# Root and reciprocal of four norms on 4 partitions x 128 tokens, spread back into PSUM by products

## What is computed

```
def rms_norm(x, gain=None):
    xf = x.astype(jnp.float32)
    y = xf * lax.rsqrt(jnp.mean(xf * xf, axis=-1, keepdims=True) + EPS)
    ...
def modulate(x, shift, scale):
    return x * (1 + scale) + shift
    ...
    for i in range(DEPTH):
        ax = modulate(rms_norm(hx, norm_mix[i]), sh1, sc1)
        ...
        hx = hx + g1 * yx
        fx = modulate(rms_norm(hx, norm_ffn[i]), sh2, sc2)
        hx = hx + g2 * swiglu(fx, ffn_w1[i], ffn_w3[i], ffn_w2[i])
    ...
        f = jnp.square(jax.nn.relu(h @ w_up[l])) @ w_down[l]
        x = x + rms_norm_2(f, ffn_post_norm[l])
```

## Time and profile before

| | |
|---|---|
| median of 3 runs | 2210.89 us (2209.84 to 2211.0) |
| span of the profiled execution | 2209.8 us |
| TensorE busy | 2159.8 us, 98% |
| VectorE busy | 1174.9 us, 53% |
| ScalarE busy | 752.9 us, 34% |
| granted TensorE clock | nine tenths or more in every one of 40 slices |
| loads and stores | 232.55 MB, 105 GB/s on average |

### The profile page before, as it was taken

How to read it: one execution, slowest core, us unless ns; L and a number is a source line. 1 busy time by engine, 2 the same in 40 slices (tenths; PEclk the granted TensorE clock), 3 DMA queues, 4 the chain that set the end, 5 groups by cost and what they waited for, 6 DMA issues and landing times.

```text
span 2209.8 us, 26001 instructions
## 1 busy us (share of the span) xinstructions
PE 2159.8 (98%) x10000; PEld 1756.9 (80%) x10000; DVE 1174.9 (53%) x1536; ACT 752.9 (34%) x1012; POOL 25.1 (1%) x52
## 2 busy tenths in 40 slices
PE   8999999999999999999999999999989998999998
PEld 4888888888788888878888888888658986888886
DVE  6665646556877323454663233357878657422424
ACT  4332322323522122332332212235665634313322
POOL 0000000000000000000000000000000000000000
PEclk9999999999999999999999999999999999999999
DMA  7342323313377222222222222232101111222221
GB/s 306 112 148 76 131 92 109 114 57 147 115 287 289 103 100 95 77 96 95 96 96 95 95 96 95 95 110 92 64 1 39 39 58 57 95 96 94 96 102 51
DMA packets 33170, 232.55 MB, mean 105 GB/s; under 512 B 3792, under 2 KB 4176, under 8 KB 5840
## 3 DMA queue, kind: packets, MB, share of 16 engines
q1 hardware_dynamic: 26336, 185.62, 23.6%
q0 software_dynamic: 5760, 41.95, 5.1%
q10 hardware_dynamic: 1008, 4.07, 0.5%
HBM read 229.52 MB, written 2.10 MB: 105 GB/s over the span
## 4 chain that ended last, share of the span: by engine, by line
PE 87%; DVE 7%; ACT 3%; issue 2%; DMA 1%; SPq 0%; ACTq 0%; DVEq 0%
PE PS L548 27%; PE PS L549 27%; PE PS L550 27%; DVE normed L1763 1%; PE PS L1076 1%; ACT w_hi L1213 1%; DVE act_lo L1755 1%; PE PS L1066 1%; PE PS L607 1%; DVE w_lo L1742 1%; PE PS L581 1%; DMA x<-x_t 1%; DVE act_lo L1772 0%; DVE rstd L1751 0%; PE PS L911 0%
## 5 line engine op out<-in xcount | busy, mean ns | idle before, releaser
L1742 DVE TENSOR_TENSOR w_lo<-raw,w_hi 128x2048 fp32r<-128x2048 f32 x162 | 371.1, 2291 | 546.0 <-ACT w_hi L1213 545.9
L1213 ACT ACTIVATE w_hi<-raw 128x2048 fp32r<-128x2048 f32 x162 | 310.2, 1915 | 982.6 <-PE PS L550 979.0
L548 PE MATMUL PS<-act_hi,w_hi 128*128 128x512 f32 x1584 | 624.0, 394 | 19.3 <-DVE act_lo L1772 10.1
L550 PE MATMUL PS<-act_hi,w_lo 128*128 128x512 f32 x1584 | 619.0, 391 | 0.0
L549 PE MATMUL PS<-act_lo,w_hi 128*128 128x512 f32 x1584 | 618.9, 391 | 0.0
L548 PEld LDWEIGHTS PS<-act_hi,w_hi 128*128 128x128 f32 x1584 | 298.9, 189 | 89.2 <-issue 15.8
L550 PEld LDWEIGHTS PS<-act_hi,w_lo 128*128 128x128 f32 x1584 | 298.8, 189 | 63.0
L549 PEld LDWEIGHTS PS<-act_lo,w_hi 128*128 128x128 f32 x1584 | 299.2, 189 | 61.8 <-issue 1.0
L548 PE MATMUL PS<-hid_hi,w_hi 128*128 128x512 f32 (+1 forms) x672 | 262.0, 390 | 1.0 <-ACT sg L1700 0.9
L549 PE MATMUL PS<-hid_lo,w_hi 128*128 128x512 f32 (+1 forms) x672 | 261.4, 389 | 0.0
L550 PE MATMUL PS<-hid_hi,w_lo 128*128 128x512 f32 (+1 forms) x672 | 261.4, 389 | 0.0
(11 more groups left out here) (429 smaller groups left out, 2472.7 us busy)
## 6 DMA issues: line engine op xcount, KB each, us to landing
raw<-slabs SPq DMA_DIRECT2D x162, 1024.0 KB, 4.8
ada_raw<-ada POOLq DMA_DIRECT2D x40, 1024.0 KB, 5.0
toep<-decay ACTq DMA_DIRECT2D x4, 768.0 KB, 4.3
early_raw<-ada SPq DMA_DIRECT2D x2, 1024.0 KB, 9.7
x<-x_t SPq DMA_DIRECT2D x2, 1024.0 KB, 10.5
ada_raw<-ada SPq DMA_DIRECT2D x2, 1024.0 KB, 15.5
early_raw<-ada SPq DMA_DIRECT2D x1, 2048.0 KB, 18.7
out_t<-x SPq DMA_DIRECT2D x4, 512.0 KB, 2.8
```

Source lines behind the costliest of these rows:

```text
L548: pe.matmul(o, w[0], a[0], start=first, stop=False)
L550: return pe.matmul(o, w[1], a[0], start=False, stop=last)
L1213: act.activation(w_hi[:, n % 2, :], raw[:, n % 2, :], ACT.Copy).then_inc(w_hi_done, 1)
L1742: dve.tensor_tensor(w_lo[:, k % 2, :], raw[:, k % 2, :], w_hi[:, k % 2, :].bitcast(F32), ALU.subtract).then_inc(w_lo_done, 1)
```

## The change

The sum of squares of the four norms is not spread over all partitions at first. `packed_sum` takes the 512 tokens as 4 groups of 128 and puts group j on partition j of the bank: each of the three products becomes four, with 128 moving columns and a 4-column slice of a small array quarter (zeros with one column of ones) as weights. `packed_root` takes the root of 4 x 128 numbers into root4, `spread_inverse` their reciprocal in place. `spread_root` then spreads each row over 128 partitions with a product of a unit column, broadcast to 128 columns, and puts the inverse into the same PSUM bank, from which VectorE reads it (`inverse`) in y. Since the first slab's tiles are still multiplied by rstd, ScalarE copies the bank to rstd at the head of its `first_pair` (semaphore inverse_kept), and VectorE's `first_pair` waits for that.

Three moves go with it. VectorE's remainder of slab n + 1 no longer stands ahead of the reciprocal but inside `norm_tail`, before the third y. ScalarE squares the last tile before it scales it. ScalarE's rounding of slab n + 1 stands behind the root. At the last norm the spread stands behind the second of TensorE's five x products. Semaphores are merged and renamed (spread_ready, root_inverted) and a padding is cut by the size of the new arrays. The core of the diff, leaving out renamings elsewhere:

```diff
+            def packed_sum(name, b):
+
+                q = nth(name)
+                for k, part in ((5, std[:, :]), (6, sq[:, 0, :]), (7, sq[:, 1, :])):
+                    pe.wait_ge(sq_ready, 8 * q + k + 1)
+                    pe.wait_ge(sq_used, 8 * q + k)
+                    for j in range(TT):
+                        mm = pe.matmul(PS[0:TT, b, 0:P], quarter[:, TT - 1 - j:2 * TT - 1 - j], part[:, j * P:(j + 1) * P],
+                                       start=(k == 5 and j == 0), stop=(k == 7 and j == TT - 1))
+                    mm.then_inc(sq_used, 1)
+
+            def spread_root(name, b):
+
+                pe.wait_ge(root_inverted, RH + packed.index(name) + 1)
+                for j in range(TT):
+                    at = VEC["unit"] + j
+                    mm = pe.matmul(PS[:, b, j * P:(j + 1) * P], vec[0:TT, at:at + 1].to_broadcast([TT, P]), root4[0:TT, :],
+                                   start=True, stop=True)
+                mm.then_inc(spread_ready, 1)
...
                     if s == at_sum:
                         pe.wait_ge(banks, freed[2])
-                        gathered_sum(nth(name), 6)
+                        packed_sum(name, 6)
+                    if s == at_sum + 1:
+                        spread_root(name, 6)
...
                 for k in range(PE_TILES):
+                    if k == 2:
+                        spread_root("last", 7)
                     pe.wait_ge(f_done, FIN.index(k) + 1)
...
+            def packed_root(name, b, bias=eps[0:TT, 0:1]):
+
+                act.wait_ge(sq_used, 8 * nth(name) + 8)
+                act.activation(root4[0:TT, :], PS[0:TT, b, 0:P], ACT.Sqrt, bias=bias, scale=1.0 / D).then_inc(std_ready, 1)
...
             def first_pair(n, seen, step, func=ACT.Silu):
 
+                act.activation(rstd[:, :], bank(6), ACT.Copy).then_inc(inverse_kept, 1)
                 after_static(n)
...
                     act.wait_ge(made, before + s + 1)
-                    scaled(name, s, k)
-                    if s == KT - 1:
-                        after_static(last_slab)
+                    if s < KT - 1:
+                        scaled(name, s, k)
                     square(nth(name), s, x[:, k, :])
-                root(nth(name), T, D, 6)
+                scaled(name, KT - 1, order[KT - 1])
+                packed_root(name, 6)
+                after_static(last_slab)
...
+            def spread_inverse(name, b):
+
+                dve.wait_ge(std_ready, nth(name) + 1)
+                dve.reciprocal(root4[0:TT, :], root4[0:TT, :]).then_inc(root_inverted, 1)
+                dve.wait_ge(spread_ready, nth_spread(name))
+                return bank(b)
...
                 if inverse is None:
-                    inverse = rstd
-                    dve.wait_ge(std_ready, nth(name) + 1)
-                    link(dve.reciprocal(rstd[:, 0:width], std[:, 0:width]))
+                    inverse = spread_inverse(name, 6)
...
+                def second_slab(k):
+
+                    if k == 2:
+                        static_rest(n + 1)
...
             if has("ffn0"):
                 scaled_rest("ffn0", KT - 1, FIN[-1])
-                static_rest(FFN0 + 1)
-                norm("ffn0", 2, 0, 3)
+                norm("ffn0", 2, 0, 3, FFN0)
```

More of the change, by code:

```diff
@@ L393, in build @@
         rope_step = sem("rope_step")
[L394 removed]
+        root_inverted = sem("root_inverted")
         o_scaled = sem("o_scaled")
@@ L399, in build @@
         gathered = ("ffn0", "mix1", "ffn1", "post2", "last")
+        packed = ("ffn0", "mix1", "ffn1", "last")
+        spreads = ["ffn0", "mix1", "ffn1", "final", "pre2", "ffn2", "last"]
         split = ["mix0", "ctx", "ffn0_x", "ffn0", "mix1_x", "mix1", "ffn1_x", "ffn1", "pre2", "ffn2"]
@@ L1976, in head @@
                 dve.wait_ge(ostd_ready, h + 1)
-                dve.reciprocal(rstd[:, :], std[:, :]).then_inc(orstd_done, 1)
-                dve.wait_ge(orstd_done, h + 1)
+                dve.reciprocal(rstd[:, :], std[:, :]).then_inc(root_inverted, 1)
+                dve.wait_ge(root_inverted, h + 1)
                 for e in range(RVT):
@@ L2187, in _ @@
             if has("ffn1"):
-                static_rest(FFN1 + 1)
-                norm("ffn1", 4, 1, 3)
+                norm("ffn1", 4, 1, 3, FFN1)
                 first_pair(FFN1, FT + KT, "ffn1")
@@ L2581, in _ @@
                 dve.wait_ge(f_done, KT)
-                inverse_root("last")
+                inverse = spread_inverse("last", 7)
                 for k in range(KT + 1):
```

71 lines of the change are left out of this document (38 added, 33 removed).

## The result

The changed kernel takes **2214.48 us** (median of 20 runs, 2212.75 to 2215.97), the kernel before 2210.94 us (20 runs, 2209.71 to 2212.58): a ratio of 1.0015 with a 95% interval of 1.0009 to 1.0022. It is slower by 0.15%, within the 0.2% that were called no change. The forecast was 2214.5. The profiled execution spans 2212.0 us against 2209.8, so this one execution is 2.2 us longer while the medians lie 3.5 apart. That difference of 1.3 us became the main question.

The account below looks back on a forecast made before the run. VectorE's train and then ScalarE were taken to set TensorE's restarts. ffn0 1.25, mix1 0.9, ffn1 1.25 and last 0.2 gave +3.6 us, forecast 2214.5 us; own range 2213.3 to 2216.0, overall range 2211.2 to 2217.0.

Parts of the forecast that it names:

- (a): Packed sums at each norm: twelve products of 128 columns replace three of 512, 0.15 us later, bounds 0 and 1.
- (b): ScalarE's root on 4 x 128 at each norm: 0.34 us against 0.69 for 512 columns, bounds 0 and 0.455.
- (c): VectorE's reciprocal on 4 x 128: 0.95 us against 3.35 for 512 columns, cost following columns; bounds 0.35 and 1.75.
- (d): Spread by four TensorE products: 1.16 us until VectorE can read, 0.89 of TensorE's stream; bounds 0.6 and 1.8.
- (e): Slab subtraction moved into VectorE's train before y2: costs 2.08 us, train ends 0.75 later; TensorE's pair still ends before Silu.
- (f): ScalarE's copy of bank 6 to rstd before the slab rounding: 0.50 us, ScalarE being the path from there on.
- (h): VectorE's y reads PSUM instead of SBUF: costs nothing by the rows, 65 ns more per y by the skill.
- the rival on it: PSUM reads stop successive y steps overlapping in VectorE's train at three places: 1.9 us on top, 2216.4 us, chance 0.08.
- dear small products: Rival: packed sums and spread cost 0.6 us more a place, in the chain to y0: 2216.9 us, chance 0.12.
- short chain that is shorter: Rival: reciprocal 0.35 and spread 0.6 bring y0 another 1.15 us forward: about +0.5 us, 2211.4 us, chance 0.10.
- released by TensorE's own pair: Sign of being wrong: waits before the restarts end with TensorE's own pair, not with VectorE's train and then ScalarE.
- The rest that was to be shown: Signs: subtraction between second and third y, TensorE waiting for Silu at ffn0, for subtraction at mix1, no idle before facc.

Follow-up runs that it names:

- moves alone: The kernel before with only VectorE's slab subtraction moved inside the y train, ahead of the third y, at ffn0, mix1 and ffn1: 2217.05 us against 2211.44.
- group 1: Two kernels made from the one before: one with only the moved subtraction, 2217.05 us, one with only the added ScalarE copy, 2212.3 us, both against 2211.44.
- copy alone: The kernel before plus one unread ScalarE copy of PSUM bank 6 at the head of first_pair at ffn0, mix1 and ffn1: 2212.3 us against 2211.44.
- spread first: The changed kernel with the last norm's spread ahead of all five x products instead of behind the second: 2217.14 us against 2210.94 for the kernel before.
- four tiles: The changed kernel with TensorE adding four output tiles instead of five, VectorE the other four: 2213.85 us, ratio 1.0013 to the kernel before.
- three norms: The changed kernel, packed only at ffn0, mix1 and last, old orders, earlier copy, TensorE adding four tiles, unread products at ffn0 and mix1: 2208.7 us against 2211.41.
- moves undone: The changed kernel with the subtraction back ahead of the reciprocal, the slab rounding and last scaled tile back in place: 2211.59 us against 2211.44 for the kernel before.
- copy early: The changed kernel with ScalarE's bank copy between the second and third rounding of act_hi, the third y waiting for it: 2213.31 us against 2211.44.
- two norms: The changed kernel with the root packed at ffn0 and mix1 only, the three old orders back and the copy earlier: 2207.99 us against 2210.94.

## Why the prediction was right, and where it was not

The number and the range held: 2214.48 against 2214.5. By its steps:

- **(a) packed sums.** Forecast 0.15 us later, measured 0.04 (the third sum starts at 568.90 + 1.18 + 0.17 = 570.25 against 570.21), and with the shorter step to the root nothing at all: root at 571.33 against 571.36. The eight passes of four columns cost what the two of 512 do. The term was mis-sized by 0.15.
- **(b), (c), (d) root to y.** Forecast 2.63, measured 2.70: root 0.36 (forecast 0.34), reciprocal 0.94 (0.95), spread 1.15 (1.16). Cost follows the columns, also on four partitions. y0 is 1.44 us earlier; forecast 1.33.
- **(e) the moved subtraction.** Forecast 2.08; moves alone gave 2.08 and 2.06 at ffn0 and ffn1, and 2.46 at mix1, where a longer low clock came on top (group 1). In the changed kernel the train ends 0.61 us later, forecast 0.75, the difference being (a).
- **(f) the copy.** Forecast 0.50, measured 0.48 on ScalarE. But the prediction took ScalarE for the path from there on, as the profile's Silu at the restart suggests, and by the end times it was VectorE's subtraction that held the kernel before, by 0.2 us (group 1). So the term is about 0.3 at ffn0 and ffn1 (0.32 and 0.34 for the copy alone), not 0.50.
- **(h) PSUM reads.** y from PSUM starts its successor after 0.66 us (578.27 to 578.93), as from SBUF. The overhead that the Trainium skill states (Perfetto Trace Analysis, Optimizing Scalar/DVE Operations) is not seen in these rows, and the rival on it falls. So do the dear small products and the short chain that is shorter.
- **The sum.** Forecast 1.25 + 0.9 + 1.25 + 0.2 = 3.6 at the places, measured 0.97 + 0.78 + 0.98 + 0.25 = 2.98, too large by 0.6. Of the 0.28 us at ffn0 about half is the train (0.61 against 0.75) and half the slack that the copy had (0.18).
- **The step that failed** is (e)'s sentence on TensorE: "Its pair took 12.65 us (577.91 to 590.56) and would end near 591.3". The 12.65 us held a stretch at the 1.2 GHz level. In the changed kernel TensorE idles 1.53 us ahead of the pair, not 2.30, the clock stays up, and the pair ends at 590.13. So the idle time moved from ahead of the pair, where a fall of the clock was covered by ScalarE and VectorE, to ahead of the restart (0.69 to 2.03 us), where it is on the path. The prediction saw the low clock in the window and took it as a given length. It was not given in the old order either: the copy alone, with 2.27 us of idle time ahead of the pair, kept its clock up and idled 2.01 us ahead of the restart. What the change did is make the high clock in the pair the rule: behind the 1.53 us it fell in none of the profiles. The missing term, at ffn0, is 0 in the changed kernel's profile and 1.6 in those of spread first and four tiles, whose code is the same there. By luck it came near the 0.6 that the other terms had too much: the median came out at +3.5 where the sum had 3.6, and part of that is the fall in the attention stage, in which the two kernels' runs differ by how often it comes (3 of 20 against 7 of 20 in the lowest group).
- **ffn1.** The prediction said that it would be wrong if the restart was released by TensorE's own pair. At ffn1 it is a tie: forecast pair 1138.9 and Silu 1139.2, measured both at 1138.9 (1140.46 less the 1.58 us gathered ahead of it), and Silu holds TensorE by the last 0.06 us. The forecast there was 0.3 too much, by the train and the copy as at ffn0; the pair is the whole cost when the copy or the moves are taken away.
- **The rest that was to be shown** came as told: the subtraction between the second and third y, Silu's release at ffn0, the subtraction's at mix1, and no idle time before the facc products.

## What to carry to other kernels

A step that is moved out of a wait costs its full length wherever the engine that it moves to is busy: here 2.1 us a place, more than the 1.4 that the shorter chain gave. Ask of each idle stretch of TensorE which side of it is covered: where hidden work gets faster, by a shorter wait or by a clock that stays up, the wait ahead of the work on the path gets longer, and a slow clock can come behind it. When a profile names one releaser, compare the ends of all that the engine waits for: two that end within 0.02 us of each other are both the path, and shortening or delaying one of them is not worth its length. Where the times of a kernel come in groups, compare the lowest group and the sum of the changed places before medians; and an unread product in an idle stretch of some 2 us can be worth more than the change in layout: one took 1.6 us off the median of three norms, where the packed root gained 1.1 at its best place.

## What the hardware showed that was not expected

- **The clock falls behind some idle times of about 2 us, not in every run.** With 2.00 to 2.03 before the restart at ffn0 it stayed up in the changed kernel, the copy alone and the moves undone, and fell in spread first and in four tiles; with 1.86 to 1.92 at mix1 it stayed up in four profiles and fell in the moves undone; with 2.33 in the attention stage it fell in eight of twelve. Behind 1.70 to 1.73 us (moves alone at ffn1, copy early and two norms at ffn0 and mix1) it fell in none. The slow products start 0.5 to 1.5 us after the restarts at ffn0 and mix1, and cost about 1.6 us. The Trainium skill (TensorE: Matmul & The Clock Gate, Part 1: The HAM clock gate) says that the clock follows the engine's recent activity and that the point at which it rises varies from run to run. The traces agree with the first: in the longest idle time, the 7.31 us before 1832.71 in the kernel before, the clock was down in all 14 profiles. The second the page says of the rise; here it is the falls that vary so. The upper group of the kernel before (2212.4 to 2212.6) was not profiled, so whether the same restarts are slow in it stays open.
- **A product that nobody reads costs nothing there and holds the clock:** ffn0 and mix1 stand at 0.90 to 0.99 and 0.78 to 0.81 with it as without, and three of them brought the scatter of a 2213 us kernel from 3.2 to 0.6 us.
- **Small products cost no more:** a group of four products of 128 columns with four weight columns takes 1.18 us to the next group's start (567.72 to 568.90); a product of 512 columns with 128 weight columns had taken 1.24 (568.97 to 570.21).
- **A reciprocal on 4 x 128 takes 0.94 us**, on the line of 6.25 ns a column through 128 x 512 (3.35) and 128 x 256 (1.75): four partitions cost what 128 do.
